# Powers of a strictly triangular matrix, and the steps that sum them, on the columns and rows that are not zero by structure

## What is computed

```python
f32 = jnp.float32
...
def gated_delta(q, k, v, beta, g, s0):
    ...
    C = min(DN_CHUNK, L)
    ...
    gamma = jnp.exp(jnp.where(causal, G[..., :, None] - G[..., None, :], -jnp.inf))
    kb = kc * bc[..., None]
    a = jnp.where(strict, jnp.einsum('bhncd,bhnsd->bhncs', kb, kc) * gamma, 0.0) + jnp.eye(C, dtype=kc.dtype)
    solve = lambda rhs: lax.linalg.triangular_solve(a, rhs, left_side=True, lower=True, unit_diagonal=True)
    u = solve(vc * bc[..., None])
    w = solve(kb * jnp.exp(G)[..., None])
    attn = jnp.einsum('bhncd,bhnsd->bhncs', qc, kc) * gamma
    ...
    def step(s, inp):
        u_i, w_i, attn_i, qg_i, kd_i, gl_i = inp
        v_new = u_i - jnp.einsum('bhcd,bhdv->bhcv', w_i, s)
        o_i = jnp.einsum('bhcd,bhdv->bhcv', qg_i, s) + jnp.einsum('bhcs,bhsv->bhcv', attn_i, v_new)
        s = s * gl_i[..., None, None] + jnp.einsum('bhcd,bhcv->bhdv', kd_i, v_new)
        return s, o_i
    ...
```

## Time and profile before

| | |
|---|---|
| median of 3 runs | 1658.73 us (1657.37 to 1659.74) |
| the profiled execution | 1663.34 us |
| its span, first to last instruction | 1661.6 us |
| mean granted clock of TensorE in it | 0.908 |
| PE busy, matmuls | 1418.0 us, 85% of the span |
| VectorE, ScalarE, GpSimd busy | 827.4, 333.9, 235.0 us |
| PE's share of the chain that ended last | 65%, then DMA 21%, VectorE 7%, ScalarE 4% |
| head loop, first start of L1112 to the end of the last head | 66.8 to about 950 us |

### The profile page before, as it was taken

How to read it: one execution, slowest core, us unless ns; L and a number is a source line. 1 busy time by engine, 2 the same in 40 slices (tenths; PEclk the granted TensorE clock), 3 DMA queues, 4 the chain that set the end, 5 groups by cost and what they waited for, 6 DMA issues and landing times.

```text
span 1661.6 us, 20978 instructions
## 1 busy us (share of the span) xinstructions
PE 1418.0 (85%) x6824; PEld 811.9 (49%) x6824; DVE 827.4 (50%) x1742; ACT 333.9 (20%) x901; POOL 235.0 (14%) x356
## 2 busy tenths in 40 slices
PE   5799999999999999999999878866887878888791
PEld 4557558466485575765846754532332323233230
DVE  1386476774865857748667522462322323222225
ACT  3122123122221231222212311100111101111112
POOL 2210111021101210111012100013111111111100
PEclk9899799998998999989999879867998989899895
DMA  8821020130210302102101240169999999999985
GB/s 190 152 53 39 27 68 23 38 79 27 53 38 27 90 2 71 45 27 53 38 27 39 115 162 40 47 242 291 420 411 415 403 413 398 403 387 417 401 331 187
DMA packets 126880, 277.79 MB, mean 167 GB/s; under 512 B 21500, under 2 KB 95158, under 8 KB 102134
## 3 DMA queue, kind: packets, MB, share of 16 engines
q1 hardware_dynamic: 103990, 196.21, 33.3%
q10 hardware_dynamic: 10704, 66.06, 11.0%
q0 software_dynamic: 12160, 15.19, 2.9%
HBM read 272.43 MB, written 30.62 MB: 182 GB/s over the span
## 4 chain that ended last, share of the span: by engine, by line
PE 65%; DMA 21%; DVE 7%; ACT 4%; issue 2%; SPq 0%; ACTq 0%; DVEq 0%; POOLq 0%; POOL 0%
DMA arena<-in_w_up 16%; PE PB L1128 13%; PE PB L1146 10%; PE PB L1482 9%; PE PB L1152 7%; PE PB L1406 4%; DMA arena<-in_w_gate 3%; PE PB L1230 2%; PE PB L1123 2%; PE PB L1258 2%; DVE arena L1628 1%; PE PB L1121 1%; PE PB L1346 1%; PE PB L1337 1%; PE PB L1085 1%
## 5 line engine op out<-in xcount | busy, mean ns | idle before, releaser
L1482 PE MATMUL PB<-arena 128*64 128x512 f32 x1024 | 268.9, 674 | 87.2 <-DMA arena<-in_w_up 71.6
L1128 PE MATMUL PB<-arena 128*128 128x512 f32 x512 | 224.0, 595 | 0.0
L1482 PEld LDWEIGHTS PB<-arena 128*64 128x64 f32 x1024 | 77.6, 154 | 250.5 <-issue 153.4
L2000 DVE TENSOR_SCALAR arena<-arena 128x256 f32<-128x256 f32 x32 | 9.5, 296 | 340.4 <-ACT arena L993 340.2
L1152 PE MATMUL PB<-arena 128*128 128x128 f32 x1280 | 167.6, 286 | 6.2 <-ACT arena L871 5.5
L1146 PE MATMUL PB<-arena 128*128 128x384 f32 x512 | 170.8, 487 | 0.0
L1152 PEld LDWEIGHTS PB<-arena 128*128 128x128 f32 x1280 | 156.8, 199 | 14.9 <-ACT arena L871 7.4
L1128 PEld LDWEIGHTS PB<-arena 128*128 128x128 f32 x512 | 96.0, 190 | 118.6 <-issue 118.1
L932 ACT ACTIVATE arena<-PB 128x512 f32<-128x512 f32 (+3 forms) x116 | 59.9, 520 | 396.4 <-PE PB L1490 224.3
L1502 PE MATMUL PB<-arena 128*64 128x512 f32 x512 | 118.6, 605 | 11.1 <-issue 9.6
L1146 PEld LDWEIGHTS PB<-arena 128*128 128x128 f32 x512 | 95.4, 190 | 63.2 <-issue 3.8
(11 more groups left out here) (433 smaller groups left out, 2025.6 us busy)
## 6 DMA issues: line engine op xcount, KB each, us to landing
arena<-in_w_gate SPq DMA_DIRECT2D x64, 1024.0 KB, 11.5
arena<-in_w_down SPq DMA_DIRECT2D x64, 1024.0 KB, 19.0
arena<-in_w_up ACTq DMA_DIRECT2D x60, 1024.0 KB, 14.8
arena<-in_w_in SPq DMA_DIRECT2D x58, 512.0 KB, 6.2
Sb<-in_state_dn SPq DMA_DIRECT2D x8, 512.0 KB, 4.0
out<-Sb POOLq DMA_DIRECT2D x8, 512.0 KB, 3.9
arena<-in_w_out SPq DMA_DIRECT2D x1, 4096.0 KB, 12.3
arena<-in_w_up SPq DMA_DIRECT2D x4, 1024.0 KB, 9.2
```

Of the source, the lines that this page charges most:

```text
L1128: last = mm(PB[g][:, :], wch[:, c, g, :], hT[:, c, 0:TP], start=c == 0, stop=c == KC - 1)
L1482: last = mm(gu_bank[a][half[k], :], xT[:, a, c, half[k]], wgu[a][:, k, :, c, :], start=c == 0, stop=c == KC - 1)
```

## The change

N is strictly triangular, so the first 2^k subdiagonals of its power 2^k are zero. `wide(k)` is the number of columns (of rows, for the transpose) that can be other than zero: 128 for k = 0, then 126, 124, 120, 112, 96, 64 for k = 1 to 6. `tall(k)` is that of the power before, `wide(k - 1)`.

- `square(k)`: the first product moves only `wide(k)` columns of `PW` (128 before) and contracts over `tall(k - 1)` rows; the weights keep their 128 columns. The second takes `wide(k - 1)` columns of `PW` as weights and writes as many rows; 128 columns of `PT` move as before.
- `grow(k)`: the weights are `wide(k)` columns of `PW`, and the moving side is the last `wide(k)` columns of `Tt`.
- `power(k)` copies 4 x `wide(k)` elements on each of 128 partitions. `powt(k)` copies on `tall(k)` partitions, 512 elements each. `growt(k)` adds 4 x `wide(k)` elements on `wide(k)` partitions.

The number of instructions, their order on every engine, and all waits and DMAs stay as they are.

```diff
--- before.py
+++ after.py
@@ -457,6 +457,12 @@
         gu_bank = (PB[2], PB[6])
         rows_of = [P] * NP + [TS]
 
+        def wide(k):
+            return P if k == 0 else P - 2 ** k
+
+        def tall(k):
+            return P if k == 0 else wide(k - 1)
+
         def rank_of(n):
             return PB[4][:, n * 64:(n + 1) * 64] if n < NP else PB[3][:, (n - NP) * 64:(n - NP + 1) * 64]
         LV = 6
@@ -872,7 +878,8 @@
 
                 def power(k):
                     act.wait_ge(s_lev_p, h * LV + k)
-                    act.activation(PW[:, k % 2, :, :], PB[0][:, :].rearrange("p (n k) -> p n k", n=NP), ACT.Copy).then_inc(s_ev_p, 1)
+                    w = wide(k)
+                    act.activation(PW[:, k % 2, :, 0:w], PB[0][:, :].rearrange("p (n k) -> p n k", n=NP)[:, :, 0:w], ACT.Copy).then_inc(s_ev_p, 1)
 
                 def probs(n):
                     lo = P if n == 0 else 0
@@ -1203,9 +1210,15 @@
                         pe.wait_ge(s_ev_p, h * LV + (k - 1))
                         pe.wait_ge(s_ev_pt, h * (LV - 1) + (k - 1))
                     a = (k - 1) % 2
-                    each(0, PT[:, a, :, :], PW[:, a, :, :]).then_inc(s_lev_p, 1)
+                    w, r = wide(k), tall(k - 1)
+                    for n in range(NP):
+                        last = mm(PB[0][:, n * P:n * P + w], PT[0:r, a, n, :], PW[0:r, a, n, 0:w], start=True, stop=True)
+                    last.then_inc(s_lev_p, 1)
                     if k < LV:
-                        each(1, PW[:, a, :, :], PT[:, a, :, :]).then_inc(s_lev_pt, 1)
+                        w = wide(k - 1)
+                        for n in range(NP):
+                            last = mm(PB[1][0:w, n * P:(n + 1) * P], PW[0:r, a, n, 0:w], PT[0:r, a, n, :], start=True, stop=True)
+                        last.then_inc(s_lev_pt, 1)
 
                 def grow(k):
 
@@ -1215,7 +1228,10 @@
                         pe.wait_ge(s_kvr_done, h * 3 + 3)
                     else:
                         pe.wait_ge(s_ev_t, h * LV + (k - 1))
-                    each(2, PW[:, k % 2, :, :], Tt).then_inc(s_lev_t, 1)
+                    w = wide(k)
+                    for n in range(NP):
+                        last = mm(PB[2][0:w, n * P:n * P + w], PW[:, k % 2, n, 0:w], Tt[:, n, P - w:P], start=True, stop=True)
+                    last.then_inc(s_lev_t, 1)
 
                 def scores(n):
                     lo = P if n == 0 else 0
@@ -1682,11 +1698,13 @@
                 tt(Tt, PT[:, 0, :, :], ident[:, :].unsqueeze(1).to_broadcast([P, NP, P]), ALU.add).then_inc(s_Tt0_done, 1)
                 def powt(k):
                     dve.wait_ge(s_lev_pt, h * (LV - 1) + k)
-                    cp(PT[:, k % 2, :, :], v4(1)).then_inc(s_ev_pt, 1)
+                    w = tall(k)
+                    cp(PT[0:w, k % 2, :, :], v4(1)[0:w]).then_inc(s_ev_pt, 1)
 
                 def growt(k):
                     dve.wait_ge(s_lev_t, h * LV + k)
-                    tt(Tt, v4(2), Tt, ALU.add).then_inc(s_ev_t, 1)
+                    w = wide(k)
+                    tt(Tt[0:w, :, P - w:P], v4(2)[0:w, :, 0:w], Tt[0:w, :, P - w:P], ALU.add).then_inc(s_ev_t, 1)
 
                 def softmax(n):
                     lo = P if n == 0 else 0
```

## The result

The changed kernel took 1651.5 us (median of 6 runs, 1650.04 to 1655.1) against 1659.24 us for the kernel before (6 runs too). The ratio is 0.9941, 95% interval 0.9915 to 0.9967: faster by 7.7 us. The forecast was 1669.6, slower. 1651.7 stood in the first rival, for an even row of heads with one long tail. The time came out and the reason did not: in the profile there is no even row and no long tail, for which the same sum has 1645.8. So that match is luck.

A forecast was written before the change was run, and what follows sets the result against it. Bound by PE in eight heads under an unsettled clock: median 1658.73 us, less 7.0 of work, plus 17.9 for three more long low-clock tails, gave 1669.6 us; forecast's own range 1662 to 1677, full range 1648 to 1682.

The forecast's parts named there:

- the first rival: Head loop: heads find another even row, one long tail at most; 1651.7 us, or 1645.8 with none; chance 0.31.
- even row: Heads 1 to 6 of the kernel before each last about 109.19 us; the forecast said the change ends this.
- long tail: State matmuls to next head's start at low clock, as in head 0 before; priced at 5.96 us each.
- the same sum: Time with n long tails: 1658.73 - 7.0 + 5.96 x (n - 1); 1645.8 us for none.
- The work: Full-clock saving per head: -0.45 - 0.10 - 0.11 - 0.22 = -0.88 us, -7.0 for eight heads.
- grow(6): PE, behind the state matmuls: 128 to 64 columns, eight passes at 0.056 us, -0.45 us a head.
- power(5) and power(6): ScalarE copies directly ahead of the chain: 128 and 256 elements fewer, -0.11 and -0.22 us a head.
- the three: grow(1) to grow(3) on PE's chain: 2, 4 and 8 columns fewer, together 0.10 us a head saved.
- growt(6): VectorE addition losing 256 elements: no gain, since it already ends before PE needs it, and not late either.
- two places: Clock falls behind the state matmuls' start: 1.94 us in head 0 (long), 2.80 us in heads 1 to 7 (recovered).
- even chance: Each head equally likely to have a long tail: about four of eight, three more than before, +17.9 us.
- the thinner tail: Narrowed grow(6) thins PE's work where the clock falls; as third rival, six to eight long tails, 1681.5 to 1693.4 us, chance 0.10.

The follow-up runs named there:

- the second execution: The kernel before, unchanged, executed and profiled once more: 1654.7 us.
- the first pair of profiles: First profiled executions of the kernel before, 1663.34 us, and of the changed kernel, 1652.77 us; the second pair repeats both unchanged, 1654.7 and 1646.5 us.

## Why the prediction was wrong, and where it was right

**The work was right.** -0.88 us a head was forecast; -0.86 is what the chains show. Term by term: grow(6) -0.38 on the chain (forecast -0.45; its passes take 0.058 us start to start against 0.056 taken, but at its ends 0.15 is left, where it was 0.09). power(5) and power(6) -0.11 and -0.22 as forecast. Of the other 0.15, grow(2) and grow(3) are 0.09; grow(1), which lies ahead of square(3), gives 0.02 (forecast for the three: 0.10). The rest is spread over the groups of square and what lies between. square stays at 0.11 us a pass from start to start with 64 moving columns as with 126: nothing, as forecast, save that its groups of eight end up to 0.05 earlier. For growt(6), VectorE's timeline says it ended at 272.68, before L1336 let PE go on at 273.10:

```profile
272.26 0.42 DVE L1707 TENSOR_TENSOR arena<-PB,arena 64x256 f32<-64x256 f32 x1 [0.38 <-PE PB L1233]
```

**That the even row breaks was right.** It did, and it did with eight passes more in the kernel before; with eight passes more in the changed kernel, which is nearly the old length, nearly the old row came back. But other repeats took its place, of three heads or of two, where the forecast had none.

**The step that failed** is the count: "I know two places, one of each kind. That is little, and I take from it an even chance for a head: of eight, about four long." It put +17.9 us into the sum; none of 16 heads of the changed kernel had a long tail. The two places seen were 0.86 us apart, and I drew them as two halves. In the tails sorted above, of 59 with a fall, 8 came in a stretch of 0.5 us where seven were long, and 46 in a stretch of 1.0 us where none was. The heads are no separate draws either: once a kernel's heads repeat, its falls do, four long ones of eight in the kernel before with eight passes more, none with the change. I had no way to read from one profile which it would be. An even chance was the wrong size for it, and the forecast's sign hung on that alone. The base of the sum was unsure too: it took the median of before to hold one long tail, and the second execution, without any, took 1654.7 us.

**Not foreseen** was a head without any fall in its tail. It takes 15.50 us there, 1.0 to 1.4 less than a tail that is low for 3.4 us. The changed kernel had three such heads in one profile and one in the other. With the low stretches in the other parts of the heads this made heads 1 to 6 shorter by 6.54 us in the first pair of profiles and by 7.1 in the second, where the work gives 5.2. In the first pair the spans differ by 10.5 us: -5.04 in head 0 (the long tail gone, a longer start), -6.54 in heads 1 to 6, -1.13 ahead of the loop and +2.25 from head 7 on.

**That the thinner tail would hurt was right in kind, wrong in size.** With grow(6) wide again fewer tails had a fall (6 of 16, against 12 of 16), and the 3 us of work that it costs were not seen. So the narrowing of grow(6) gained nothing measurable here until the state matmuls were made wider; then it gained 4.1 us by the medians.

What stays open: why a fall's place goes with its length and why one at 3.75 us was long, why a kernel's heads settle in one pattern or another, what PE's waits have to do with the falls, and the time of the whole change with a clock that never falls, since falls at the starts of heads and behind the reciprocals remained in every kernel.

## What to carry to other kernels

When the clock moves within a loop, price the work at the full clock, and find out where the falls land before putting a price on the clock: profile the kernel twice, and once with a known delay in each turn. Where passes take the same time however many columns move, as the 16 passes with 128 weight columns did here, more columns can be streamed at no cost; that was worth 12 to 17 us in the changed kernel (against its two medians) and 11 in the one before, more than the 7.7 of leaving out the zeros. Work taken out of a stretch where PE streams little may come back as clock.

## What the runs showed of the hardware

Passes with equal weights and moving columns follow the width closely: 0.058 us start to start at 64, 0.085 at 96, 0.098 at 112, 0.105 at 120, 0.110 at 126, which is 0.87 to 0.91 ns a column, at 126 as at 64. With 128 weight columns a pass takes 0.11 us whether 8, 64 or 126 columns move. And with 36 instead of 8 moving columns on average in those 16 passes, at the same 1.74 us, the clock fell in none of 24 tails of the three changed kernels that had them, against 12 of 16 of the changed kernel without; with ScalarE's order turned and 8 columns it fell in 2 of 8.
